# Third layer, head-pair scores: one fp32 product against three rounded products of split queries and keys

## The chip, the cores and the metric

The kernel runs on one core of a Trainium2 chip. The metric is the device time of one launch in microseconds (us). The core has TensorE (PE, matrix products; PEld is its weight load), VectorE (DVE), ScalarE (ACT), GpSimd (POOL) and the queues that issue DMAs (SP). Each engine works through its own instructions in order and waits on semaphores that others raise.

## What is computed

Three layers over 512 tokens of width 1024 (a gated linear attention, a sparse attention, and a hybrid layer with stick-breaking attention). The change is in the third layer's attention, which the reference computes so, in 16 heads of 64 dimensions:

```python
proj = h @ w_in
q, k, v, z_a, u, z_b, m_a, m_b = jnp.split(proj, offs, axis=-1)
...
z = jnp.einsum('bhqd,bhkd->bhqk', qb, kb).astype(jnp.float32) * SB_SCALE
mask = k_pos < q_pos
log_1m_beta = jnp.where(mask, -jax.nn.softplus(z), 0.0)
suffix = lax.cumsum(log_1m_beta, axis=3, reverse=True) - log_1m_beta
w = jnp.where(mask, jnp.exp(jax.nn.log_sigmoid(z) + suffix), 0.0)
outs.append(jnp.einsum('bhqk,bhkd->bhqd', w.astype(vb.dtype), vb))
...
p_a = (attn * jax.nn.silu(z_a)) @ w_branch_a
```

## The kernel before

**Products.** Every large matrix product is three products of rounded parts: both operands are split into a high part (rounded to the type fp32r) and a low part (what is left of it), and high x high, high x low and low x high are added up in PSUM. Weights come in chunks of 256 columns, numbered c; ACT rounds the high part (`split_high`), POOL subtracts it for the low part (line 600). The third layer's chunks start at C_H = 40: four chunks each for a group of four heads, q, k, v, z; from C_MA = 56 on come other columns. A chunk's product has two halves m = 0 and 1 of 24 matmuls with 512 columns each (line 1224), or 48 with 256 (line 1215, for v).

**Two banks for the products.** During the head pairs the products of all chunks share PSUM banks 0 and 1, half m in bank m (`shared=True`). So half m of chunk c + 1 must not start before half m of chunk c has been taken out of the bank. The semaphores `bank_free` say that; in the kernel before, the take by ACT (`taker`, lines 1084 to 1095) raises them.

**The pairs.** The heads run in 8 pairs p = 0 to 7. Beside pair p, PE computes two chunks of a later group, q and k in the even pairs 0, 2, 4, then v and z in the odd ones 1, 3, 5 (pairs 6 and 7 have chunks of m_a). The order on PE in one pair is written by hand: the pair's scores with their masks (`head_scores`), both halves of chunk c, half 0 of chunk c + 1, the sums of the logarithms (`head_sums`, line 1760), half 1 of chunk c + 1, and the products with the values (`head_values`, line 1774). The two heads of a pair sit in partitions 0 to 63 and 64 to 127, so each score matmul uses 64 rows, and the two heads use different rows of the array. A head's scores are four blocks of keys st = 0 to 3 with 512, 384, 256 and 128 query columns. They are plain fp32: the profile shows two matmuls for each one written.

**What DVE and ACT do beside it.** For each pair: DVE caps the scores in three groups (line 2290), ACT takes Exp and Ln of each (1111, 1114), then DVE makes for each group a maximum, a rounding and a low part (lines 2294 to 2296), on whose last one `head_sums` waits. Behind these DVE makes the low part of the last pair's output (`pair_part`, line 2284) and multiplies this pair's values by the gate (line 2301). The outputs of pair p live in `br_hi[:, p]` and `br_lo[:, p]`, which nothing uses before the pair is done.

Of the kernel before, what the change touches and what calls it, by code (L numbers as in the profile page):

```python
# [14 lines left out]
F32 = mybir.dt.float32  # L15
F32R = mybir.dt.float32r
# [4 lines left out]
P = 128  # L21
D = 1024
S = 512
# [14 lines left out]
NG, NHG, NDH = 4, 4, 64  # L38
# [33 lines left out]
def build_program(nc, A, out):  # L72
    es = ExitStack()
    with es:
        mem = [nc.sbuf_base + 64 - nc.sbuf_base % 64]

        def sb(name, shape, dt=F32):

            n = 1
            for x in shape[1:]:  # L80
                n *= x
            n *= 4
            t = nc.alloc_sbuf_tensor_at(name, list(shape), dt, offset=mem[0])
            mem[0] += (n + 31) // 32 * 32
            assert mem[0] <= nc.sbuf_usable_end, (name, mem[0], nc.sbuf_usable_end)
            return t

        def sem(name):
            return es.enter_context(nc.semaphore(name))

        banks = es.enter_context(nc.psum_tensor("banks", [P, 8, S], F32))
        bank = [banks[:, i, :] for i in range(8)]
# [143 lines left out]

        mem[0] = arena
        br_hi, br_lo = sb("br_hi", [P, KT, S], F32R), sb("br_lo", [P, KT, S], F32R)
        qh, kh = sb("qh", [P, 2, 2, S]), sb("kh", [P, 2, 2, S])
        vh, zh = sb("vh", [P, 2, TT, CW]), sb("zh", [P, 2, 2, S])  # L240
        mix_a = sb("mix_a", [P, KT, S])

# [14 lines left out]
        rows3 = over("rows3", [P, 2, D], qh)  # L257
# [10 lines left out]
        bank_full = [sem(f"bank_full{i}") for i in range(4)]  # L268
        bank_free = [sem(f"bank_free{i}") for i in range(4)]
# [43 lines left out]
        z_full, zc_ready, e_ready, l_ready, sp_ready = sem("z_full"), sem("zc_ready"), sem("e_ready"), sem("l_ready"), sem("sp_ready")  # L313
        mix_sigmoid = sem("mix_sigmoid")
        a2_scored = sem("a2_scored")
        tri_full, w_ready, hv_full, head_gated = sem("tri_full"), sem("w_ready"), sem("hv_full"), sem("head_gated")
        pair_high, pair_low = sem("pair_high"), sem("pair_low")
        d_ready, d_high, d_low, mix_full, mix_taken = sem("d_ready"), sem("d_high"), sem("d_low"), sem("mix_full"), sem("mix_taken")
# [10 lines left out]
        C_H, C_MA, C_U, C_BA, C_ZB, C_MB, C_MIX, C_BB, C_OUT = 40, 56, 60, 64, 68, 72, 76, 77, 81  # L329
# [20 lines left out]
        def blocks(x, a, st, skip=0):  # L350

            at, c0 = zone(a, st)
            return x[:, at, c0 + skip * P:c0 + (TT - st) * P]
# [5 lines left out]
        z_banks = banks[:, 3:8, :]  # L359
# [295 lines left out]
        def _(act):  # L655
# [55 lines left out]
            def step2(c, take, ahead=True):  # L711
                if ahead:
                    split_high(c + 1, (c + 1) // 2, (c + 1) % 2)
                u = c % 2
                for m in range(2):
                    act.wait_ge(bank_full[2 * u + m], c // 2 + 1)
                    take(m, bank[2 * u + m]).then_inc(bank_free[2 * u + m], 1)
# [341 lines left out]
            for u in range(NUNIT + 1):  # L1059
# [4 lines left out]
                q = z_piece_end(u)  # L1064
# [4 lines left out]
                if u in split_next:  # L1069
                    c = split_next[u]  # L1070
# [11 lines left out]
            def taker(c):  # L1082

                s, kind = (c - C_H) // 4 % 2, (c - C_H) % 4
                if c >= C_MA:
                    return lambda m, b: act.activation(mix_a[:, 2 * (c - C_MA) + m], b, ACT.Copy)
                return (lambda m, b: act.activation(qh[:, s, m], b, ACT.Copy, scale=NDH ** -0.5),
                        lambda m, b: act.activation(kh[:, s, m], b, ACT.Copy),
                        lambda m, b: act.activation(vh[:, s, 2 * m:2 * m + 2], b.rearrange("p (t n) -> p t n", t=2), ACT.Copy),
                        lambda m, b: act.activation(zh[:, s, m], b, ACT.Silu))[kind]  # L1090

            def take3(c, m):
                b = 2 * (c % 2) + m
                act.wait_ge(bank_full[b], c // 2 + 1)
                taker(c)(m, bank[m]).then_inc(bank_free[b], 1)

            def pair_split(p):
                act.wait_ge(head_gated, p + 1)
                act.activation(br_hi[:, p], gated[:, p % 2], ACT.Copy).then_inc(pair_high, 1)

            for c in range(C_H, C_H + 4):
                step2(c, taker(c), ahead=(c > C_H))
            for p in range(HH // 2):
                c = C_H + 4 + 2 * p
                if p % 2 == 0:
# [55 lines left out]
            for c in range(C_OUT, C_END):  # L1161
                if c + 1 < C_END:
                    split_high(c + 1, (c + 1) // 2, (c + 1) % 2)
                j = c - C_OUT
# [9 lines left out]
        def _(pe):  # L1174
# [175 lines left out]
            for t in range(TT):  # L1350
                pe.wait_ge(start_scaled, t + 1)
                for k in range(KT):
                    mm = pe.transpose(start_bank(k)[:, t * P:(t + 1) * P], xn_tok[:, t, k * P:(k + 1) * P], ident[:])
# [109 lines left out]
            for h in range(GH):  # L1463
                if h < GH - 1:
                    updates(h + 1)
                for e in range(2):
# [76 lines left out]
            for k in range(KT):  # L1543
# [3 lines left out]
                mm = pe.matmul(bank[2 * u + 1][:], w_hi[:, u, k, 0:2 * NDH], act_hi[:, k, :], start=(k == 0), stop=(k == KT - 1))  # L1547
# [9 lines left out]
            for g in range(NG):  # L1557
                for m in range(2):
                    mm = pe.matmul(bank[6][:, g * NDH:(g + 1) * NDH],
                                   hid4[:, m, g * P:(g + 1) * P],  # L1560
                                   w2v[:, m, :], start=(m == 0), stop=(m == 1))
            mm.then_inc(cmp_full, 1)
            pe.wait_ge(gates_t_ready, 1)
            for t in range(TT):
                mm = pe.matmul(bank[7][:, t * 48:(t + 1) * 48], gate_parts[:, t * P:(t + 1) * P], pair_ident[:], start=True, stop=True)
# [108 lines left out]
            for j in range(2):  # L1674
                c = C_NQ + 2 + j
# [3 lines left out]
            c = C_NZ  # L1679
# [3 lines left out]
            c = C_NZ + 1  # L1683
# [22 lines left out]
            for row, col in enumerate((gain_mod, mod)):  # L1706
                for k in range(KT):
                    mm = pe.matmul(bank[mod_row_bank(row, k // 4)][:, k % 4 * P:(k % 4 + 1) * P],
                                   col[:, k:k + 1].broadcast_to([P, P]), ident[:], start=True, stop=True)
# [7 lines left out]
            def rows3(a):  # L1717
                return slice(a * NDH, (a + 1) * NDH)

            def score(p, a, st, start):  # L1720

                s, tile = p // 2 % 2, p % 2
                return pe.matmul(blocks(z_banks, a, st), kh[rows3(a), s, tile, st * P:(st + 1) * P],  # L1723
                                 qh[rows3(a), s, tile, st * P:S], start=start, stop=False, skip_group_check=True)

            def score_mask(a, st):

# [3 lines left out]
            def head_scores(p):  # L1731

                if p:
                    pe.wait_ge(w_ready, 3 * p)
                score(p, 0, 2, start=True).then_inc(a2_scored, 1)
                score(p, 1, 1, start=True)
                score(p, 0, 1, start=True)
                pe.wait_ge(a2_scored, p + 1)
                score(p, 1, 2, start=False)
                score(p, 0, 3, start=False)  # L1740
                score(p, 1, 3, start=False)
                for st in (1, 3):
                    score_mask(0, st)
                    mm = score_mask(1, st)
                mm.then_inc(z_full, 1)
                score_mask(0, 2)
                score_mask(1, 2).then_inc(z_full, 1)
                score(p, 0, 0, start=True)
                score(p, 1, 0, start=True)
                score_mask(0, 0)  # L1750
                score_mask(1, 0).then_inc(z_full, 1)

# [27 lines left out]
            for p in range(HH // 2):  # L1780
                c = C_H + 4 + 2 * p
# [11 lines left out]
            c, u = C_MIX, C_MIX % 2  # L1793
# [4 lines left out]
            for tile in range(KT):  # L1798
                if tile >= 4:
                    pe.wait_ge(mix_taken, tile - 3)  # L1800
                for i in range(2):
                    k = tile // 2 * 2 + i
                    for n, (w, x) in enumerate(((w_hi, br_hi), (w_lo, br_hi), (w_hi, br_lo))):
                        mm = pe.matmul(bank[4 + tile % 4], w[:, u, k, tile % 2 * P:(tile % 2 + 1) * P], x[:, k, :],  # L1804
                                       start=(i == 0 and n == 0), stop=(i == 1 and n == 2))
# [19 lines left out]
        def _(dve):  # L1825
# [456 lines left out]
            def pair_part(p):  # L2282
                dve.wait_ge(pair_high, p + 1)
                dve.tensor_tensor(br_lo[:, p], gated[:, p % 2], br_hi[:, p].bitcast(F32), ALU.subtract).then_inc(pair_low, 1)

            for p in range(HH // 2):
                for i, g in enumerate((1, 2, 0)):

                    dve.wait_ge(z_full, 3 * p + i + 1)
                    dve.tensor_scalar(group(ln_z, g), group(z_banks, g), CAP, None, ALU.min).then_inc(zc_ready, 1)  # L2290
                for i, g in enumerate((1, 2, 0)):

                    dve.wait_ge(l_ready, 3 * p + i + 1)
                    link(dve.tensor_tensor(group(ln_z, g), group(ln_z, g), group(z_banks, g), ALU.max))
                    link(dve.tensor_copy(group(sp_hi, g), group(ln_z, g)))
                    dve.tensor_tensor(group(sp_lo, g), group(ln_z, g), group(sp_hi, g).bitcast(F32),
                                      ALU.subtract).then_inc(sp_ready, 1)
                if p:
                    pair_part(p - 1)
                dve.wait_ge(hv_full, p + 1)  # L2300
                dve.tensor_tensor(gated[:, p % 2], bank[2], zh[:, p // 2 % 2, p % 2], ALU.mult).then_inc(head_gated, 1)  # L2301
            pair_part(HH // 2 - 1)
# [144 lines left out]
```

## Time and profile before

| | us |
|---|---|
| median of 3 runs | 1287.04 (1286.7 to 1287.11) |
| the profiled execution | 1288.17 |
| its span, first to last instruction | 1286.5 |
| PE busy | 1241.5 (97%) |
| DVE busy | 647.8 (50%) |
| ACT busy | 574.5 (45%) |
| POOL busy | 350.7 (27%) |
| the 8 head pairs in the trace | 736.5 to 1002.9 |

Around the span lie 1288.17 - 1286.5 = 1.7 us. PE's records overlap: a matmul's record is longer than the step to the next one, since its end lies about 0.16 us behind the last column; steps between starts tell the rate.

### The profile page before, as it was taken

Reading aid. Unit: us, or ns where it says so; the run is one execution under the profiler, and the core shown is the slowest. Engines: PE = TensorE matmul, PEld = TensorE weight load, DVE = VectorE, ACT = ScalarE, POOL = GpSimd, SP = SyncE. Lnnn points to the kernel's source line nnn. Section 1 sums busy time; section 2 is a strip of 40 time slices with the busy share of each in tenths; the row PEclk is TensorE's granted clock in tenths of the full one; section 3 lists DMA queues with packets and bytes.
Section 4 is the critical chain, followed back from the end, with each engine's and each line's share of the span. In section 5 each row is a group of like instructions: output and inputs, shape, how many; then the busy total and the mean of one; then the engine's idle time right before and its main releaser. Section 6 shows DMA issues by size and latency. Waiting matters only on the chain.

```text
span 1286.5 us, 19286 instructions
## 1 busy us (share of the span) xinstructions
PE 1241.5 (97%) x7710; PEld 1031.7 (80%) x7710; DVE 647.8 (50%) x1214; ACT 574.5 (45%) x1082; POOL 350.7 (27%) x174
## 2 busy tenths in 40 slices
PE   7999998999899999999999999999999999999998
PEld 6799876998878765566799888788877788888897
DVE  4487544475756657798837033333333491102434
ACT  4434212353532256788845445444444311434333
POOL 3344401210014302100020432322222454444441
PEclk9999997999999999999999999999999999999999
DMA  7326400816566412100022322222222223333221
GB/s 225 119 67 196 131 1 33 261 44 193 153 123 123 103 33 66 25 11 2 2 67 66 99 66 66 66 66 66 66 67 66 66 98 98 98 109 103 77 89 66
DMA packets 131201, 111.69 MB, mean 87 GB/s; under 512 B 38802, under 2 KB 128016, under 8 KB 131120
## 3 DMA queue, kind: packets, MB, share of 16 engines
q1 hardware_dynamic: 129600, 106.84, 28.3%
q10 hardware_dynamic: 1520, 3.72, 1.3%
q8 instruction: 57, 0.93, 0.3%
q14 instruction: 24, 0.20, 0.0%
HBM read 104.78 MB, written 2.10 MB: 83 GB/s over the span
## 4 chain that ended last, share of the span: by engine, by line
PE 71%; issue 14%; DVE 7%; POOL 4%; ACT 3%; DMA 0%; ACTq 0%; POOLq 0%; SPq 0%; DVEq 0%
PE banks L1224 33%; PE banks L1215 8%; PE banks L1247 5%; POOL w_lo L600 4%; PE banks L1760 3%; PE banks L1612 3%; PE banks L1629 3%; PE banks L1644 3%; PE banks L1312 2%; PE banks L1667 2%; PE banks L1723 2%; DVE w_lo L1863 2%; PE banks L1774 1%; PE banks L1804 1%; PE banks L1191 1%
## 5 line engine op out<-in xcount | busy, mean ns | idle before, releaser
L600 POOL TENSOR_TENSOR w_lo<-raw,w_hi 128x1024 fp32r<-128x1024 f32 x138 | 339.8, 2483 | 844.7 <-ACT w_hi L675 832.6
L1224 PE MATMUL banks<-act_hi,w_hi 128*128 128x512 f32 x704 | 278.4, 395 | 5.0 <-DVE w_lo L1863 4.9
L1224 PE MATMUL banks<-act_hi,w_lo 128*128 128x512 f32 x704 | 276.1, 392 | 0.0
L1224 PE MATMUL banks<-act_lo,w_hi 128*128 128x512 f32 x704 | 276.0, 392 | 0.0
L675 ACT ACTIVATE w_hi<-raw 128x1024 fp32r<-128x1024 f32 (+1 forms) x164 | 162.8, 1042 | 134.6 <-PE banks L1224 87.8
L1224 PEld LDWEIGHTS banks<-act_hi,w_hi 128*128 128x128 f32 x704 | 133.3, 189 | 34.3 <-issue 6.3
L1224 PEld LDWEIGHTS banks<-act_lo,w_hi 128*128 128x128 f32 x704 | 133.3, 189 | 28.2
L1224 PEld LDWEIGHTS banks<-act_hi,w_lo 128*128 128x128 f32 x704 | 133.4, 189 | 27.3
L1215 PE MATMUL banks<-w_hi,act_hi 128*128 128x256 f32 x384 | 109.1, 284 | 0.0
L1215 PE MATMUL banks<-w_hi,act_lo 128*128 128x256 f32 x384 | 108.7, 283 | 0.0
L1215 PE MATMUL banks<-w_lo,act_hi 128*128 128x256 f32 x384 | 108.7, 283 | 0.0
L1039 ACT ACTIVATE prob<-prob,wstat 128x128 f32<-128x128 f32 (+3 forms) x128 | 70.8, 554 | 34.0 <-DVE wstat L2192 33.8
L2301 DVE TENSOR_TENSOR tmp<-banks,zh 128x512 f32<-128x512 f32 x8 | 5.5, 692 | 141.7 <-PE banks L1774 141.7
L1215 PEld LDWEIGHTS banks<-w_hi,act_hi 128*128 128x128 f32 x384 | 73.7, 192 | 0.2 <-issue 0.2
L1215 PEld LDWEIGHTS banks<-w_lo,act_hi 128*128 128x128 f32 x384 | 73.7, 192 | 0.0
L1215 PEld LDWEIGHTS banks<-w_hi,act_lo 128*128 128x128 f32 x384 | 73.7, 192 | 0.0
L1629 PEld LDWEIGHTS banks<-ident,prob 128*128 128x128 f32 x320 | 35.7, 141 | 33.1 <-issue 25.2
L1247 PE MATMUL banks<-w_hi,act_hi 128*128 128x256 f32 x192 | 56.2, 293 | 4.7 <-POOL w_lo L600 2.5
L2192 DVE CUSTOM_DVE_ANT_0 prob<-banks,key_mask 128x128 f32<-128x128 f32 (+3 forms) x128 | 57.0, 482 | 3.6 <-PE banks L1612 3.4
L1247 PE MATMUL banks<-w_lo,act_hi 128*128 128x256 f32 x192 | 55.5, 289 | 0.0
L1247 PE MATMUL banks<-w_hi,act_lo 128*128 128x256 f32 x192 | 55.4, 289 | 0.0
L1629 PE MATMUL banks<-ident,prob 128*128 128x128 f32 x320 | 48.1, 280 | 5.7 <-ACT probT L1052 3.7
(380 smaller groups left out, 2405.5 us busy)
## 6 DMA issues: line engine op xcount, KB each, us to landing
raw<-w_in SPq DMA_DIRECT2D x32, 1024.0 KB, 5.7
raw<-gla_w_in SPq DMA_DIRECT2D x11, 1024.0 KB, 5.3
raw<-nsa_w_in SPq DMA_DIRECT2D x33, 256.0 KB, 4.4
raw<-nsa_w_in SPq DMA_DIRECT2D x6, 1024.0 KB, 5.7
raw<-gla_w_out SPq DMA_DIRECT2D x4, 1024.0 KB, 10.2
ada_first<-w_ada SPq DMA_DIRECT2D x4, 1024.0 KB, 9.1
raw<-nsa_w_out SPq DMA_DIRECT2D x16, 256.0 KB, 4.4
raw<-w_branch_a SPq DMA_DIRECT2D x4, 1024.0 KB, 5.1
```

The costliest lines, as they stand in the source:

```text
L600: pool.tensor_tensor(w_lo[:, u, k], raw[:, u, k], w_hi[:, u, k].bitcast(F32), ALU.subtract).then_inc(lo_done, 1)
L675: act.activation(w_hi[:, u, k, 0:n], raw[:, u, k, 0:n], ACT.Copy).then_inc(hi_done, 1)
L1039: act.activation(p, p, ACT.Exp, scale=-1.0, bias=wstat[:, u % 4, 0, half:half + 1], accum_out=wstat[:, u % 4, 1, half:half + 1]).then_inc( ...
L1215: mm = pe.matmul(b[:, t * CW:(t + 1) * CW], x[:, k, tok], w[:, u, k, :], start=(k == 0 and n == 0), stop=(k == KT - 1 and n == 2))
L1224: mm = pe.matmul(b[:], w[:, u, k, m * P:(m + 1) * P], x[:, k, :], start=(k == 0 and n == 0), stop=(k == KT - 1 and n == 2))
L1247: mm = pe.matmul(zone, x[:, k, tok], w[:, u, k, :], start=(start and n == 0), stop=(stop and n == 2), skip_group_check=True)
L1312: mm = pe.matmul(bank[2 * u + m][:, tok], w[:, u, k, m * P:(m + 1) * P], x[:, k, tok], start=(half == 0 and k == 0 and n == 0), stop=(k == ...
L1612: mm = pe.matmul(bank[2 * (u % 2) + half][:, 0:keys], qT[rows, i, t * P:(t + 1) * P], kT[rows, i // 4, 0:keys], start=True, stop=True)
L1629: mm = pe.transpose(bank[4 + half][:, k * P:(k + 1) * P], prob[:, u % 3, half, k * P:(k + 1) * P], ident[:])
L1644: mm = pe.matmul(bank[6][half * NDH:(half + 1) * NDH, 0:P], v_tok2[:, k, w, g * NDH:(g + 1) * NDH], probT[:, u % 2, half, k * P:(k + 1) * ...
L1760: mm = pe.matmul(blocks(z_banks, a, st, skip=jt - st), (tri_r if jt == st else minus_r)[:], blocks(part, a, jt), start=False, stop=(jt == ...
L2192: last = dve.tensor_tensor_reduce(prob[:, u % 3, half, 0:keys], bank[2 * (u % 2) + half][:, 0:keys], key_mask[:, S - keys:S], -1.0, -NEG, ...
```

## The change

`qh` and `kh`, the queries and keys of a group of four heads, are now fp32r, so ACT rounds them as it takes them from the banks. DVE makes the low parts from the same bank: bank times the scale minus `qh` into `br_hi[:, p]`, bank minus `kh` into `br_lo[:, p]`, in the tiles where the pair's own output will come later. A score block is then three fp32r matmuls (n = 0, 1, 2): high keys with high queries, high keys with low queries, low keys with high queries. The banks of q and k are given free by DVE's instruction, no longer by ACT's, which raises the new semaphore `qk_high`. The low parts of the first group are made before pair 0, those of the later groups during pairs 0, 2 and 4: the queries' two halves behind the pair's softplus chain, the keys' two halves behind `pair_part`.

```diff
-        qh, kh = sb("qh", [P, 2, 2, S]), sb("kh", [P, 2, 2, S])
+        qh, kh = sb("qh", [P, 2, 2, S], F32R), sb("kh", [P, 2, 2, S], F32R)
...
-                taker(c)(m, bank[m]).then_inc(bank_free[b], 1)
+                taken = qk_high if (c - C_H) % 4 < 2 and c < C_MA else bank_free[b]
+                taker(c)(m, bank[m]).then_inc(taken, 1)
...
-            def score(p, a, st, start):
+            def score(p, a, st, n, start):
...
+                k = (kh[:, s, tile], kh[:, s, tile], br_lo[:, p])[n]
+                q = (qh[:, s, tile], br_hi[:, p], qh[:, s, tile])[n]
+                return pe.matmul(blocks(z_banks, a, st), k[rows3(a), st * P:(st + 1) * P], q[rows3(a), st * P:S],
+                                 start=(start and n == 0), stop=False, skip_group_check=True)
...
+                for n in range(3):
+                    mm = score(p, 0, 2, n, start=True)
+                    score(p, 1, 1, n, start=True)
+                mm.then_inc(a2_scored, 1)
+                score(p, 0, 1, 0, start=True)
                 pe.wait_ge(a2_scored, p + 1)
...
+            def query_low(j, m, b):
+
+                dve.wait_ge(qk_high, 4 * j + m + 1)
+                dve.scalar_tensor_tensor(br_hi[:, 2 * j + m], b, NDH ** -0.5, qh[:, j % 2, m].bitcast(F32), ALU.mult,
+                                         ALU.subtract).then_inc(bank_free[2 * (C_H % 2) + m], 1)
+
+            def key_low(j, m, b):
+
+                dve.wait_ge(qk_high, 4 * j + m + 3)
+                dve.tensor_tensor(br_lo[:, 2 * j + m], b, kh[:, j % 2, m].bitcast(F32), ALU.subtract)                    .then_inc(bank_free[2 * ((C_H + 1) % 2) + m], 1)
...
+                if p % 2 == 0 and p < 6:
+                    for m in range(2):
+                        query_low(p // 2 + 1, m, bank[m])
                 if p:
                     pair_part(p - 1)
+                if p % 2 == 0 and p < 6:
+                    for m in range(2):
+                        key_low(p // 2 + 1, m, bank[m])
                 dve.wait_ge(hv_full, p + 1)
```

How the instructions stand on DVE in pair 2, from the last group of the softplus chain (ln_z, sp_hi, sp_lo) on, first in the kernel before. `tmp` is the tile of the gated values.

```order
L2294 TENSOR_TENSOR ln_z_154<-ln_z_154,banks 128x1024 [waits l_ready]
L2295 CAST sp_hi_155<-ln_z_154 128x1024 [waits dve_chain]
L2296 TENSOR_TENSOR sp_lo_163<-ln_z_154,sp_hi_155 128x1024 [waits dve_chain]
L2284 TENSOR_TENSOR br_lo_148<-tmp_62,br_hi_147 128x512 [waits pair_high]
L2301 TENSOR_TENSOR tmp_62<-banks,zh_152 128x512 [waits hv_full]
```

The same place in the changed kernel:

```order
L2326 TENSOR_TENSOR ln_z_154<-ln_z_154,banks 128x1024 [waits l_ready]
L2327 CAST sp_hi_155<-ln_z_154 128x1024 [waits dve_chain]
L2328 TENSOR_TENSOR sp_lo_163<-ln_z_154,sp_hi_155 128x1024 [waits dve_chain]
L2306 SCALAR_TENSOR_TENSOR br_hi_147<-banks,qh_149 128x512 [waits qk_high] x2
L2301 TENSOR_TENSOR br_lo_148<-tmp_62,br_hi_147 128x512 [waits pair_high]
L2312 TENSOR_TENSOR br_lo_148<-banks,kh_150 128x512 [waits qk_high] x2
L2339 TENSOR_TENSOR tmp_62<-banks,zh_152 128x512 [waits hv_full]
```

The two queries' low parts stand behind the whole chain, the two keys' between `pair_part` and the gate.

On PE, the scores of a pair up to the first product of chunk c, in the kernel before (a shape is array columns x moving columns):

```order
L1723 MATMUL banks<-qh_149,kh_150 128x256 [waits bank_free2,bank_free1,bank_free3,bank_free0,consts3_ready]
L1723 MATMUL banks<-qh_149,kh_150 128x384 x2
L1723 MATMUL banks<-qh_149,kh_150 128x256 [waits a2_scored]
L1723 MATMUL banks<-qh_149,kh_150 128x128 x2
L1729 MATMUL banks<-maskb3_161,identb3_160 128x128 x6
L1723 MATMUL banks<-qh_149,kh_150 128x512 x2
L1729 MATMUL banks<-maskb3_161,identb3_160 128x128 x2
```

And in the changed kernel, the first block of the scores, as far as its blocks of 384 and 256 columns go:

```order
L1733 MATMUL banks<-qh_149,kh_150 128x256 [waits bank_free2,bank_free1,bank_free3,bank_free0,consts3_ready]
L1733 MATMUL banks<-qh_149,kh_150 128x384
L1733 MATMUL banks<-br_hi_147,kh_150 128x256
L1733 MATMUL banks<-br_hi_147,kh_150 128x384
L1733 MATMUL banks<-qh_149,br_lo_148 128x256
L1733 MATMUL banks<-qh_149,br_lo_148 128x384
L1733 MATMUL banks<-qh_149,kh_150 128x384
L1733 MATMUL banks<-qh_149,kh_150 128x256 [waits a2_scored]
L1733 MATMUL banks<-br_hi_147,kh_150 128x384
L1733 MATMUL banks<-br_hi_147,kh_150 128x256
L1733 MATMUL banks<-qh_149,br_lo_148 128x384
L1733 MATMUL banks<-qh_149,br_lo_148 128x256
```

The heads alternate, and the wait on `a2_scored` now stands behind the third product of head 0's 256-column block. The first matmul of half 0 of chunk c + 1 waits on lo_done and bank_free0 in both kernels; what differs is who raises bank_free0.

## Rows read from the trace of the kernel before

**Rows 1.** The page: busy time (share of the span) and instructions of each engine
```profile
PE 1241.5 (97%) x7710; PEld 1031.7 (80%) x7710; DVE 647.8 (50%) x1214; ACT 574.5 (45%) x1082; POOL 350.7 (27%) x174
```

**Rows 2.** The chain that ended last, pair 2: start us, us, what
```profile
822.98 5.54 PE banks L1760 x40
...
834.00 2.31 PE banks L1774 x16
836.31 1.60 PE banks L1723 x10
```

**Rows 3.** PE's waits over the whole span: us in total, times, longest (cut)
```profile
PE banks L1723 <- ACT zh L1090: 0.8, 1, 0.8
```

**Rows 4.** Timeline of PE, pair 2's scores: start us, us, engine, line, tiles, shape
```profile
803.18 1.67 PE L1723 MATMUL banks<-qh,kh 64*128 64x256 f32 x12
804.78 0.51 PE L1729 MATMUL banks<-maskb,identb 128*128 128x128 bf16 x6
805.22 1.13 PE L1723 MATMUL banks<-qh,kh 64*128 64x512 f32 x4
806.28 0.28 PE L1729 MATMUL banks<-maskb,identb 128*128 128x128 bf16 x2
```

**Rows 5.** Timeline of PE, the second half of the 512-column block
```profile
805.75 0.60 PE L1723 MATMUL banks<-qh,kh 64*128 64x512 f32 x2
```

**Rows 6.** Timeline of PE, head_sums of pair 1: fp32r matmuls of four widths
```profile
791.38 0.27 PE L1760 MATMUL banks<-sp_lo,minus_r 128*128 128x128 f32 x1
791.49 0.33 PE L1760 MATMUL banks<-sp_hi,tri_r 128*128 128x256 f32 x1
...
792.86 0.28 PE L1760 MATMUL banks<-sp_lo,minus_r 128*128 128x256 f32 x1
792.98 0.34 PE L1760 MATMUL banks<-sp_hi,tri_r 128*128 128x384 f32 x1
...
794.20 0.33 PE L1760 MATMUL banks<-sp_lo,minus_r 128*128 128x384 f32 x1
794.37 0.39 PE L1760 MATMUL banks<-sp_hi,tri_r 128*128 128x512 f32 x1
794.60 0.40 PE L1760 MATMUL banks<-sp_lo,tri_r 128*128 128x512 f32 x1
```

**Rows 7.** Timeline of DVE, pair 2's chain
```profile
805.22 2.95 DVE L2290 TENSOR_SCALAR ln_z<-banks 128x1024 f32<-128x1024 f32 x3 [1.23 <-PE banks L1729]
...
817.13 1.23 DVE L2296 TENSOR_TENSOR sp_lo<-ln_z,sp_hi 128x1024 fp32r<-128x1024 f32 x1
818.27 0.68 DVE L2284 TENSOR_TENSOR br_lo<-tmp,br_hi 128x512 fp32r<-128x512 f32 x1
```

**Rows 8.** Timeline of ACT and PE where chunk c + 1 of pair 2 starts
```profile
812.14 0.60 ACT L1087 ACTIVATE qh<-banks 128x512 f32<-128x512 f32 x1 [0.45 <-PE banks L1224]
...
817.38 0.39 PE L1224 MATMUL banks<-act_hi,w_hi 128*128 128x512 f32 x1
817.58 0.60 ACT L1087 ACTIVATE qh<-banks 128x512 f32<-128x512 f32 x1 [4.32 <-PE banks L1224]
```

**Rows 9.** Groups of DVE by form: xcount | busy us, mean ns | idle before
```profile
L2070 DVE SCALAR_TENSOR_TENSOR rope_q<-banks,cosT 128x512 f32<-128x512 f32 x10 | 6.9, 687 | 5.4 <-PE banks L1224 4.8 <-DVE rope_q L2071 0.5
```

**Rows 10.** Timeline, DVE releases a waiting PE
```profile
692.75 1.22 DVE L2274 TENSOR_TENSOR y_tok<-y_tok,mod_rows 128x1024 f32<-128x1024 f32 x1
...
694.03 0.33 PE L1300 MATMUL banks<-ident,y_tok 128*128 128x128 f32 x1 [0.72 <-DVE y_tok L2274]
```

**Rows 11.** Stretches around pauses of PE: us, busy (x) of five engines, PEclk, DMA share, GB/s
```profile
270.40:272.20 1.80, 0.14 (x2) 0.05 (x1) 1.80 (x4) 1.49 (x7) 0.00 (x0) 1.00 0.11 13
272.20:275.60 3.40, 3.40 (x28) 3.40 (x29) 3.06 (x4) 3.34 (x7) 0.00 (x0) 1.00 0.91 301
299.10:301.10 2.00, 0.14 (x3) 0.08 (x2) 1.39 (x2) 1.52 (x2) 0.00 (x0) 1.00 0.56 127
301.10:304.60 3.50, 3.50 (x9) 2.74 (x10) 3.25 (x6) 0.00 (x0) 0.00 (x0) 0.53 0.32 70
```

More of the change, by code:

```diff
@@ L315, in build_program @@
         a2_scored = sem("a2_scored")
+        qk_high = sem("qk_high")
         tri_full, w_ready, hv_full, head_gated = sem("tri_full"), sem("w_ready"), sem("hv_full"), sem("head_gated")
@@ L1099, in pair_split @@
                 act.activation(br_hi[:, p], gated[:, p % 2], ACT.Copy).then_inc(pair_high, 1)
-            for c in range(C_H, C_H + 4):
-                step2(c, taker(c), ahead=(c > C_H))
+            for c in range(C_H, C_H + 2):
+                if c > C_H:
+                    split_high(c + 1, (c + 1) // 2, (c + 1) % 2)
+                for m in range(2):
+                    act.wait_ge(bank_full[2 * (c % 2) + m], c // 2 + 1)
+                    taker(c)(m, bank[2 * (c % 2) + m]).then_inc(qk_high, 1)
+            for c in range(C_H + 2, C_H + 4):
+                step2(c, taker(c))
             for p in range(HH // 2):
@@ L1718, in rows3 @@
                 return slice(a * NDH, (a + 1) * NDH)
-            def score(p, a, st, start):
+            def score(p, a, st, n, start):
                 s, tile = p // 2 % 2, p % 2
-                return pe.matmul(blocks(z_banks, a, st), kh[rows3(a), s, tile, st * P:(st + 1) * P],
-                                 qh[rows3(a), s, tile, st * P:S], start=start, stop=False, skip_group_check=True)
+                k = (kh[:, s, tile], kh[:, s, tile], br_lo[:, p])[n]
+                q = (qh[:, s, tile], br_hi[:, p], qh[:, s, tile])[n]
+                return pe.matmul(blocks(z_banks, a, st), k[rows3(a), st * P:(st + 1) * P], q[rows3(a), st * P:S],
+                                 start=(start and n == 0), stop=False, skip_group_check=True)
             def score_mask(a, st):
@@ L1734, in head_scores @@
                     pe.wait_ge(w_ready, 3 * p)
-                score(p, 0, 2, start=True).then_inc(a2_scored, 1)
-                score(p, 1, 1, start=True)
-                score(p, 0, 1, start=True)
-                pe.wait_ge(a2_scored, p + 1)
-                score(p, 1, 2, start=False)
-                score(p, 0, 3, start=False)
-                score(p, 1, 3, start=False)
+                for n in range(3):
[3 more added lines that the diff above has]
+                score(p, 0, 1, 0, start=True)
+                pe.wait_ge(a2_scored, p + 1)
+                for n in range(3):
+                    if n:
+                        score(p, 0, 1, n, start=True)
+                    score(p, 1, 2, n, start=False)
+                for n in range(3):
+                    for a in range(2):
+                        score(p, a, 3, n, start=False)
                 for st in (1, 3):
@@ L1747, in head_scores @@
                 score_mask(1, 2).then_inc(z_full, 1)
-                score(p, 0, 0, start=True)
-                score(p, 1, 0, start=True)
+                for n in range(3):
+                    for a in range(2):
+                        score(p, a, 0, n, start=True)
                 score_mask(0, 0)
@@ L2284, in pair_part @@
                 dve.tensor_tensor(br_lo[:, p], gated[:, p % 2], br_hi[:, p].bitcast(F32), ALU.subtract).then_inc(pair_low, 1)
+            def query_low(j, m, b):
[6 more added lines that the diff above has]
+            for m in range(2):
+                query_low(0, m, bank[2 * (C_H % 2) + m])
+            for m in range(2):
+                key_low(0, m, bank[2 * ((C_H + 1) % 2) + m])
             for p in range(HH // 2):
@@ L2297, in _ @@
                                       ALU.subtract).then_inc(sp_ready, 1)
+                if p % 2 == 0 and p < 6:
+                    for m in range(2):
+                        query_low(p // 2 + 1, m, bank[m])
                 if p:
                     pair_part(p - 1)
+                if p % 2 == 0 and p < 6:
+                    for m in range(2):
+                        key_low(p // 2 + 1, m, bank[m])
                 dve.wait_ge(hv_full, p + 1)
```

## The prediction

> **What bounds the kernel now.** I read the page first, then the chain of work that ended last, then PE's waits, then the timelines of all engines in one head pair. PE is busy for 97% of the span, the next engine for 50% [rows 1]. In the chain, a whole pair is PE and nothing else; the three rows shown are pair 2's sums, its values and the scores of the next pair [rows 2], and the other seven pairs repeat this. Of all waits of PE, one lies at the head pairs: 0.8 us for the last z half ahead of pair 0 [rows 3]. So in these 266 us every PE column counts, and nothing else does until it makes PE wait. Two questions follow: how long are the scores on PE, and does a new wait arise.
>
> **The scores on PE.** In pair 2 they stand in two blocks. The first runs from 803.18 to the masks at 804.78, 1.60 us; the 512-column one from 805.22 to 806.28, 1.06 us [rows 4]. Together 2.66 us.
>
> Before: a score is two matmuls, and from the first pair of 512-column ones (805.22) to the second (805.75) are 0.53 us [rows 4, 5]. The two heads start together (two matmuls in one row of the timeline), so they run side by side. Of the 1.06 us, 512 columns take four column times (4 x 512 / 2.4 = 853 ns at the granted full clock of 2.4 GHz), and some 0.2 us are left: the first load of weights and the drain before the masks, which use the whole array. I split them 0.10 and 0.10.
>
> After: three fp32r matmuls for each. The steps between fp32r matmuls on 128 rows are 0.11 us for 128 columns, 0.12 for 256, 0.17 for 384, 0.23 for 512 [rows 6]. No fp32r matmul on 64 rows with two heads side by side is in the trace, so this is to be bounded.
> - 512-column block: 3 x 0.227 + 0.20 = 0.88 us, against 1.06: 0.17 less.
> - First block: the heads go 256 beside 384, then 384 beside 256, then 128 beside 128. In step with the longer one that is 6 x 0.173 + 3 x 0.11 = 1.37, plus 0.20 for load and drain: 1.57. The wait on a2_scored comes on top: it stands behind the third 256-column product, whose record ends 0.28 us after its start (as at 792.86 [rows 6]), and a fresh load of 0.10 follows. Head 0 runs ahead in the meantime (256 columns beside 384), so I count at most 0.1 for it. 1.6 to 1.7 us against 1.60: no change to 0.1 more.
>
> So I take 0.2 us less for the scores of a pair, nearly all in the second block, and none before the first masks, on which DVE's chain waits.
>
> Bounds: at best pure columns. Three column times in place of four make 0.21 us less in the 512-column block and, for 768 columns of a head, 0.32 less in the first: 0.53. At worst the heads don't run side by side: 2 x 3 x (0.227 + 0.173 + 0.12 + 0.11) = 3.8 us plus 0.2 to 0.4, 1.3 to 1.5 more than now. I take the middle estimate since the fp32 rows show both heads in step on the same rows of the array.
>
> One published rule speaks against the gain. The trace has the second 512-column matmul of the same rows starting 0.53 us after the first, of which 0.43 are columns and 0.10 is the first load, so the second load cost nothing [rows 5]. The Trainium skill, "TensorE: Matmul & The Clock Gate", Part 3 (The mechanism), has a load overlap a running matmul only when its row group differs; by that each of the 12 products of a head would show its load.
>
> **The added wait.** In the changed kernel, half 0 of chunk c + 1 waits for bank 0, and in pairs 0, 2 and 4 it is DVE's low part of the queries that gives it free. Before, ACT did: it took q's half 0 at 812.14 to 812.74, and PE wanted the bank at 817.38, 4.6 us later [rows 8]. But on DVE query_low is queued behind the pair's whole softplus chain. Pair 2's chain begins at 805.22 with the first masks, and its last instruction ends at 817.13 + 1.23 = 818.36 [rows 7]. The next instruction of DVE starts at 818.27, a little before that end, and takes 0.68; query_low takes its place. Its duration: 0.687 us for the same operation out of PSUM [rows 9], as long as the low part whose place it takes (0.68); I take 0.69. It ends at 818.96. A waiting PE starts 0.05 us after DVE's end (692.75 + 1.22 = 693.98 with the digits cut off, and 694.03 [rows 10]), and the load, hidden in the stream, now shows with 0.10. So the product that started at 817.38 starts streaming at 819.11: 1.73 us late. What hid ACT's take was 4.6 us of cover; what DVE's place in the queue leaves is less than none.
>
> This time is counted from the pair's first masks, so what the 512-column block saves is swallowed in these three pairs: PE comes to the bank 0.2 us sooner and waits 1.9. In pairs 0 and 4 the chain stands the same way (the odd ones have no query_low).
>
> Who waits behind it: everything on PE, whose queue is in order; nothing of that is recovered, since PE is the bound to the end. head_sums finds its inputs ready: they were 4.6 us early (818.36 against 822.98 [rows 2, 7]) and now more.
>
> **The other waits.** query_low of half 1 needs ACT's take, 817.58 to 818.18 [rows 8], which is there by 818.96; it ends at 819.65, and bank 1 is wanted only after half 0 and head_sums, 11 us on. key_low of half 0 comes while PE is in head_sums. key_low of half 1 waits for the half that ends with line 1224 at 834.00, then 0.6 for ACT's take and 0.7 of its own: done 1.3 us after, where the gate on DVE waits for head_values, 2.31 us [rows 2]: covered by 1.0. The next pair's chunk needs these banks 3 us later still. The first group's four low parts lie before pair 0, beside 22 us of v and z products; DVE is idle there. ACT's rounding costs it 0.03 us each, with ACT at 45%. All of this at nothing; if key_low were not covered it would push the gate of three pairs by some 0.3 us, still behind PE.
>
> **The sum.** Three pairs with +1.73: +5.2. Five pairs with -0.2: -1.0. Together +4.2 us, from 1288.17 to 1292.4 for the profiled execution, and from the median 1287.04 to 1291.2. The profiled one lies 1.1 above the median, all of it kept out of the difference.
>
> **The clock.** PE pauses for 1.9 us three times in a stretch where it never paused. What such pauses do to the granted clock shows in the second layer: after that from 270.4 it stayed at full, after that from 299.1 it stood at 0.53 of full for 3.5 us, near the lower of its two levels [rows 11]. 3.4 us at half speed lose 1.7. [...]
>
> **Rivals.**
> 1. As summed, no clock fall: +4.2, 1291.2 us. Range of its own 1290.2 to 1292.2.
> 2. One of the three pauses brings the clock down: +5.9, 1292.9. Two or three: +7.6 to +9.3, up to 1296.3. For it: one of the two pauses of this length in rows 11. Against: it was the longer one.
> 3. The scores gain in full, and the stall shrinks with them: the first masks come 0.32 sooner, so the chain and the bank too. 3 x (1.73 - 0.32) - 5 x 0.53 = +1.6, 1288.6: not slower than can be told. It decides at a first block of 1.3 us in place of 1.6. For it: a fourth of the column time is really gone. Against: the 0.11 us step at 128 columns [rows 6] and the wait on a2_scored.
> 4. Each product shows the load of its weights, 0.10. In the first block the nine steps have columns for 6 x 0.16 + 3 x 0.05 = 1.12 us, with nine loads and the drain 2.1, so 0.5 more; the second has 3 x (0.21 + 0.10) + 0.10 = 1.04, as now. 3 x (1.73 + 0.5) + 5 x 0.5 = +9.2, 1296.2. Against: rows 5. It is what the rule on loads above would give.
> 5. The heads run one after another: 3 x (1.73 + 1.0) + 5 x 1.3 = +14.7, 1301.7.
> 6. The wait isn't there: only if DVE took the bank ahead of its chain, which the order of its instructions rules out. It would leave 8 x -0.2 = -1.6, 1285.4.
>
> **Chances.** First 0.48; second 0.32 (one fall 0.23, more 0.09); third 0.09; fourth 0.05; fifth 0.03; sixth 0.03. The forecast is 1291.2 us. A measurement of this kernel tells 0.2%, 2.6 us, from no change: 1289.6 is the bound. Slower: 0.48 + 0.32 + 0.05 + 0.03 = 0.88. Same: the third and nearly all of the sixth, 0.11. Faster: 0.01, the far end of the sixth. The range 1289.4 to 1294.8 holds the first and one or two clock falls.
>
> **What would show it.** PE's waits get a line of 1224's successor on DVE's query_low (line 2306), 3 times, 1.7 to 1.9 us each, and head pairs 0, 2 and 4 last 1.7 longer, the others 0.2 shorter. In the stretch of each pair the first block of scores reads 1.5 to 1.7 us, the 512-column one about 0.9. query_low reads 0.69 and starts as the last low part of the chain ends. I am wrong if there is no such wait, if the first block's length is off by more than 0.2, or if the clock falls behind a pause.

## The result: 0.3% slower, by the wait on DVE's queue

| | kernel before | changed kernel |
|---|---|---|
| median | 1286.7 us (13 runs) | 1290.87 us (13 runs) |
| ratio to before | | 1.0029, 95% interval 1.0018 to 1.0040 |
| profiled execution: time, span | 1288.17, 1286.5 | 1289.53, 1287.8 |
| from pair 0's first score to the first matmul behind pair 7 | 266.33 | 270.18 |
| from there to the end | 283.66 | 283.65 |

The forecast was +4.2 us; the medians differ by 4.2, the ratio says 3.7 (2.3 to 5.1), so that the two 4.2 agree to the digit is luck. The two profiled spans differ by only 1.3 us. This is no smaller loss: the eight pairs alone take 3.85 us longer, and the stretch behind them is the same to 0.01. What is missing lies ahead of pair 0, which starts at 736.46 in one trace and at 733.96 in the other. Matmul by matmul, this distance is complete at 506 us, ahead of the third layer, and changes by less than 0.05 us from there to pair 0. So the first group's low parts, which the changed kernel makes there, cost nothing. The distance comes for the most part from the clock, which stood at half for 30.7 us of the first two layers in one trace and for 23.9 in the other. In all traces below that front part moves by some us from run to run, while the last part is 283.65 to 283.67. So I take effects from the eight pairs, and the ratios beside them.

A wait of PE in the changed kernel that the kernel before hasn't (us in total, times, longest us):

```profile
PE banks L1232 <- DVE br_hi L2306: 5.0, 3, 1.7
```

Line 1232 is the chunks' product (before: 1224), line 2306 the low part of the queries. In the kernel before only the 0.8 us of [rows 3] lay at the pairs.

The chain that ended last, in pair 2 of the changed kernel (start us, us, what):

```profile
802.22 1.51 PE banks L1733 x17
803.73 0.34 PE banks L1739 x4
804.08 0.02 issue
804.10 2.96 DVE ln_z L2322 x3
...
816.01 1.23 DVE sp_lo L2328
817.24 0.61 DVE br_hi L2306
817.85 0.04 issue
817.89 5.74 PE banks L1232 x24
```

Where [rows 2] had PE alone, the chain now leaves PE at the first masks, runs through the whole softplus chain on DVE and ACT and comes back through the queries' low part. The timelines of DVE and PE there:

```profile
816.01 1.23 DVE L2328 TENSOR_TENSOR sp_lo<-ln_z,sp_hi 128x1024 fp32r<-128x1024 f32 x1
817.15 1.28 DVE L2306 SCALAR_TENSOR_TENSOR br_hi<-banks,qh 128x512 fp32r<-128x512 f32 x2
818.35 2.49 DVE L2301 TENSOR_TENSOR br_lo<-tmp,br_hi 128x512 fp32r<-128x512 f32 x1
```
```profile
815.85 0.39 PE L1232 MATMUL banks<-act_lo,w_hi 128*128 128x512 f32 x1
817.89 0.50 PE L1232 MATMUL banks<-act_hi,w_hi 128*128 128x512 f32 x1 [1.66 <-DVE br_hi L2306]
```

The low part starts 13.05 us behind the start of the chain at 804.10, as the low part of line 2284 does in [rows 7] (818.27 - 805.22), and PE starts streaming 0.05 us after its first half is done (two halves in 1.28 us, 0.68 each, since they overlap a little). The scores of the same pair:

```profile
802.15 0.44 PE L1733 MATMUL banks<-qh,kh 64*128 64x256 f32 x2
...
803.66 0.51 PE L1739 MATMUL banks<-maskb,identb 128*128 128x128 bf16 x6
804.10 0.50 PE L1733 MATMUL banks<-qh,kh 64*128 64x512 f32 x2
804.44 0.39 PE L1733 MATMUL banks<-br_hi,kh 64*128 64x512 f32 x2
804.67 0.39 PE L1733 MATMUL banks<-qh,br_lo 64*128 64x512 f32 x2
805.00 0.28 PE L1739 MATMUL banks<-maskb,identb 128*128 128x128 bf16 x2
```

The first block takes 803.66 - 802.15 = 1.51 us (1.60 in [rows 4]), the 512-column one 0.90 (1.06). From the second to the third product are 0.23 us, the step of 128-row fp32r matmuls in [rows 6]. "x2" are the two heads.

The length of the eight pairs, from start to start, in us:

| pair | 0 | 1 | 2 | 3 | 4 | 5 | 6 | 7 | sum |
|---|---|---|---|---|---|---|---|---|---|
| before | 33.03 | 33.69 | 33.06 | 33.69 | 33.06 | 33.69 | 33.06 | 33.06 | 266.33 |
| changed | 34.76 | 33.44 | 34.73 | 33.44 | 34.77 | 33.44 | 32.78 | 32.82 | 270.18 |

Pairs 0, 2 and 4 are 1.73, 1.67 and 1.71 longer, the others 0.24 to 0.28 shorter: +5.1 and -1.3.

### The profile page after: what moved, and what is told of

Its sections match the earlier page's. It is cut to its first block, busy times and chain, and to the rows that moved or that the text cites. A ratio compares the mean times of both kernels' runs of the same rounds, so it can differ in the third digit from the quotient of the medians.

```text
span 1287.8 us, 19430 instructions
## 1 busy us (share of the span) xinstructions
PE 1236.9 (96%) x7774; PEld 1030.1 (80%) x7774; DVE 662.1 (51%) x1230; ACT 574.5 (45%) x1082; POOL 351.2 (27%) x174
## 4 chain that ended last, share of the span: by engine, by line
PE 68%; issue 14%; DVE 9%; POOL 4%; ACT 4%; ACTq 1%; DMA 0%; SPq 0%; POOLq 0%; DVEq 0%
PE banks L1232 31%; PE banks L1223 8%; PE banks L1255 5%; POOL w_lo L601 4%; PE banks L1777 3%; PE banks L1620 3%; PE banks L1637 3%; PE banks L1652 3%; PE banks L1320 2%; PE banks L1675 2%; DVE w_lo L1880 2%; PE banks L1791 1%; PE banks L1733 1%; PE banks L1821 1%; ACT w_hi L676 1%
```

## The experiments

Eight further runs: six new kernels, one of them twice, and the changed kernel again. Ratios are to the kernel before on the same chip. Its median there was 1287.6 us for the first four rows and 1287.24 us for the last four.

| kernel | eight pairs, us | against before | median | ratio, 95% interval |
|---|---|---|---|---|
| low part of the queries early | 264.34 | -2.0 | 1284.96 | 0.9979 (0.9967 to 0.9991) |
| the wait alone, old scores | 271.66 | +5.3 | 1292.72 | 1.0043 (1.0030 to 1.0057) |
| low part later | 273.00 | +6.7 | 1292.64 | 1.0040 (1.0026 to 1.0054) |
| early, heads apart | 269.60 | +3.3 | 1291.3 | 1.0034 (1.0017 to 1.0050) |
| the changed kernel again | 270.18 | +3.9 | 1290.78 | 1.0035 (1.0023 to 1.0048) |
| early, again | 264.29 | -2.0 | 1288.02 | 0.9996 (0.9979 to 1.0013) |
| early, no score wait | 263.58 | -2.7 | 1284.77 | 0.9982 (0.9969 to 0.9994) |
| early, heads in threes | 263.70 | -2.6 | 1282.13 (one run) | |

### The low part of the queries ahead of the last group

```diff
                     dve.tensor_tensor(group(sp_lo, g), group(ln_z, g), group(sp_hi, g).bitcast(F32),
                                       ALU.subtract).then_inc(sp_ready, 1)
-                if p % 2 == 0 and p < 6:
-                    for m in range(2):
-                        query_low(p // 2 + 1, m, bank[m])
+                    if i == 1 and p % 2 == 0 and p < 6:
+                        query_low(p // 2 + 1, 0, bank[0])
+                if p % 2 == 0 and p < 6:
+                    query_low(p // 2 + 1, 1, bank[1])
```

> The changed kernel with one instruction of VectorE moved: in pairs 0, 2 and 4 the low part of the queries' half 0 stands ahead of the last of the three groups of the softplus chain, no longer behind it. Everything else is as in the changed kernel. Theory A (the place in VectorE's queue is the whole loss): the low part ends 3.4 us sooner, well ahead of the product that wants bank 0; the three pauses of TensorE of 1.66 us go, the chain ends 0.7 us later and head_sums, which has over 4 us to spare, doesn't notice. The head pairs lose 3 x 1.7 = 5 us against the changed kernel and stand at 8 x -0.26 = -2.1 against the kernel before, ratio 0.9984. Rival B (the loss lies in VectorE's added work itself, or in its reads of the banks beside TensorE): as much work, so the ratio stays near 1.003. Rival C (the chain's delay moves the wait to head_sums): a wait at head_sums takes its place, ratio 1.000 or more.

DVE's timeline in pair 2, and PE's where half 0 of chunk c + 1 starts:

```profile
813.62 0.68 DVE L2306 SCALAR_TENSOR_TENSOR br_hi<-banks,qh 128x512 fp32r<-128x512 f32 x1
814.22 1.21 DVE L2326 TENSOR_TENSOR ln_z<-ln_z,banks 128x1024 f32<-128x1024 f32 x1
...
817.93 2.53 DVE L2301 TENSOR_TENSOR br_lo<-tmp,br_hi 128x512 fp32r<-128x512 f32 x1
```
```profile
815.46 0.39 PE L1232 MATMUL banks<-act_lo,w_hi 128*128 128x512 f32 x1
815.68 0.39 PE L1232 MATMUL banks<-act_hi,w_hi 128*128 128x512 f32 x1
```

The low part ends at 814.30, the product starts at 815.68 one step of 0.22 us behind the last. PE has no wait on line 2306 any more and none on the sums; its chain in pair 2 is all PE again:

```profile
801.79 1.51 PE banks L1733 x15
803.31 0.44 PE banks L1739 x6
803.75 0.90 PE banks L1733 x6
804.65 0.22 PE banks L1739 x2
804.87 16.42 PE banks L1232 x72
```

The same instructions in another place save 5.8 us in the pairs: the place was the loss. The expectation's 5 left out that the three pairs, once their length isn't set by the wait, keep the 0.25 us of the scores too. Rivals B and C fall.

Run again, beside the changed kernel:

> The run with the early low part of the queries once more, beside the changed kernel itself. Theory: 5.5 us less than the changed kernel (in the trace 270.2 against 264.3 us for the eight pairs), 2.1 less than the kernel before, ratio to it 0.998.

The eight pairs took 264.29 us, 5.9 less than the changed kernel's 270.18 beside it. The ratio, 0.9996, isn't the 0.998 expected and doesn't settle it: 6 of its 12 executions lie at 1289.3 to 1289.9 us with a mean clock of 0.984, the others at 1282.6 to 1286.7. The kernel before had such executions too (4 of 23 at 1291.5 to 1291.9 us and 0.985), only not as often; in the traces half-clock stretches ahead of pair 0 make such differences, and why this one met more of them stays open.

### The changed kernel, beside the others

> The changed kernel as it is, on the chip of the next three, so that they can be compared with it. Theory: +3.7 us against the kernel before (ratio 1.003), with the three pauses of 1.66 us in pairs 0, 2 and 4.

It came out at 1.0035, with 270.18 us in the pairs, as in its first trace.

### The wait without the new scores

```diff
-            def score(p, a, st, n, start):
+            def score(p, a, st, start):
 
                 s, tile = p // 2 % 2, p % 2
-                k = (kh[:, s, tile], kh[:, s, tile], br_lo[:, p])[n]
-                q = (qh[:, s, tile], br_hi[:, p], qh[:, s, tile])[n]
...
+                return pe.matmul(blocks(z_banks, a, st), kh[rows3(a), s, tile, st * P:(st + 1) * P].bitcast(F32),
+                                 qh[rows3(a), s, tile, st * P:S].bitcast(F32), start=start, stop=False, skip_group_check=True)
...
```

> The changed kernel with the scores in the old form: one plain fp32 product for each block, in the old order, on the rounded queries and keys. The low parts are still made and still give the banks free, but no product reads them, so the low parts are left out of the scores. Theory A: the wait without the gain. The first masks come as late as before the change, so the pause is shorter on TensorE's side by what the scores no longer save (1.4 us in place of 1.66), and the pairs 0, 2, 4 last 1.73 longer than before, the others the same: +5.2 us against the kernel before, ratio 1.0040. If the score products themselves cost anything hidden, this one would come out faster than the changed kernel; theory A has it 1.3 us slower (5 x 0.25).

```profile
PE banks L1232 <- DVE br_hi L2297: 4.4, 3, 1.5
```

Pairs 0, 2 and 4 last 34.84, 34.83, 34.83 us, 1.8 more than before, the others within 0.02 of before: +5.3 for the wait by itself. Against it the changed kernel has 1.5 less. That is what the new scores are worth while the wait sets the length of three pairs: 5 x 0.25 saved in the others, and in these three the first masks, and with them the chain, come 0.09 sooner (0.06 in pair 0).

### The low part one instruction later

```diff
-                if p % 2 == 0 and p < 6:
-                    for m in range(2):
-                        query_low(p // 2 + 1, m, bank[m])
                 if p:
                     pair_part(p - 1)
+                if p % 2 == 0 and p < 6:
+                    for m in range(2):
+                        query_low(p // 2 + 1, m, bank[m])
```

> The changed kernel with the queries' low parts one instruction later: behind pair_part. Theory A: the pause grows by that instruction's 0.68 us in the two pairs that have one (2 and 4; pair 0 has none), from 1.66 to 2.35, so +1.4 us against the changed kernel, ratio to the kernel before 1.004. If pair_part there runs beside GpSimd's split and takes 2.5 us, as it does in the changed kernel, the pauses of pairs 2 and 4 grow by 2.5 each, +5 us. Rival B: no difference to the changed kernel.

Pairs 0, 2, 4 last 34.78, 36.95 and 35.34 us. Pair 4 is 0.57 longer than in the changed kernel and pair 0, which has no `pair_part`, is the same: the pause follows the place in the queue. The 0.68 of the first theory is nearly met; the 2.5 that it allowed for isn't, since `pair_part` takes 0.68 here (the last section shows why). Pair 2 has 1.6 us more still, which the theory didn't have: +2.8 in all against the changed kernel, not +1.4. The stretches around its pause and pair 4's show why (us; busy of PE, PEld, DVE, ACT, POOL; PEclk; DMA share; GB/s):

```profile
818.10:820.40 2.30, 0.07 (x2) 0.05 (x1) 2.30 (x4) 2.24 (x3) 0.62 (x1) 1.00 0.00 0
820.40:825.00 4.60, 4.60 (x13) 3.67 (x14) 0.50 (x1) 0.24 (x1) 4.07 (x2) 0.63 0.00 0
888.50:890.70 2.20, 0.01 (x1) 0.00 (x0) 2.20 (x4) 2.15 (x3) 0.54 (x1) 1.00 0.00 0
890.70:894.10 3.40, 3.36 (x15) 2.79 (x16) 0.58 (x1) 0.33 (x1) 3.40 (x2) 1.00 0.00 0
```

Behind the pause of 2.2 us in pair 2 the granted clock is 0.63 on the mean of 4.6 us, part of it at the lower level; behind pair 4's pause of the same length it is full. The changed kernel's three pauses of 1.7 us never did this, in either of its two traces, nor the three of 1.5 us in the experiment before. In the changed kernel, pair 2:

```profile
816.20:817.90 1.70, 0.04 (x2) 0.01 (x1) 1.70 (x3) 1.63 (x3) 0.01 (x1) 1.00 0.00 0
817.90:821.30 3.40, 3.40 (x15) 2.83 (x16) 2.94 (x2) 0.86 (x1) 3.40 (x2) 1.00 0.00 0
```

The length of a pause alone doesn't tell what the clock does. In the second layer of the same trace a fall followed a pause of the same 1.7 us:

```profile
461.00:462.70 1.70, 0.16 (x2) 0.17 (x4) 1.48 (x8) 0.18 (x1) 0.00 (x0) 1.00 0.00 0
462.70:467.30 4.60, 4.60 (x19) 3.13 (x20) 2.52 (x17) 3.46 (x16) 0.00 (x0) 0.63 0.01 4
```

### The two heads apart, and in threes

Built on the early low part. All products of head 0 stand ahead of all of head 1, in both blocks:

```diff
-                for n in range(3):
-                    mm = score(p, 0, 2, n, start=True)
-                    score(p, 1, 1, n, start=True)
-                mm.then_inc(a2_scored, 1)
...
+                for n in range(3):
+                    mm = score(p, 0, 2, n, start=True)
+                mm.then_inc(a2_scored, 1)
+                for n in range(3):
+                    score(p, 0, 1, n, start=True)
+                for n in range(3):
+                    score(p, 0, 3, n, start=False)
+                for n in range(3):
+                    score(p, 1, 1, n, start=True)
                 pe.wait_ge(a2_scored, p + 1)
...
-                for n in range(3):
-                    for a in range(2):
+                for a in range(2):
+                    for n in range(3):
                         score(p, a, 0, n, start=True)
```

> As the run with the early low part of the queries, but the scores' products in another order: all of head 0's, then all of head 1's, in both blocks. Theory (the two heads run side by side only where they alternate): the first block takes 2 x 1.21 + 0.2 = 2.6 us in place of 1.51 and the 512-column block 6 x 0.227 + 0.2 = 1.56 in place of 0.90, so 1.75 us more for each pair, 14 us in all, ratio 1.009 against the kernel before. Rival (the order doesn't matter, since TensorE lets a later head's product pass): the same time as the run that it is built on.

Neither held for the first block, which took 2.18 us, not 2.6 and not 1.51; the 512-column block took 0.90, as in alternating order. The eight pairs are 5.3 us longer than with the early low part alone, not 14. The timeline in pair 2:

```profile
802.40 0.33 PE L1733 MATMUL banks<-br_hi,kh 64*128 64x384 f32 x1
802.58 0.33 PE L1733 MATMUL banks<-qh,br_lo 64*128 64x384 f32 x1
802.59 0.44 PE L1733 MATMUL banks<-qh,kh 64*128 64x384 f32 x2
802.81 0.39 PE L1733 MATMUL banks<-br_hi,kh 64*128 64x128 f32 x2
...
804.38 0.51 PE L1733 MATMUL banks<-qh,kh 64*128 64x512 f32 x2
804.72 0.41 PE L1733 MATMUL banks<-br_hi,kh 64*128 64x512 f32 x2
```

Head 0's sixth product starts at 802.58. At 802.59 starts a high x high one of 384 columns: head 1's first, the tenth in the program. Head 0's seventh to ninth, the 128-column ones, come later: the seventh is the other one of the "x2" of that row and starts at 802.75, the eighth has the row at 802.81. In the 512-column block the fourth product of the program starts beside the first (804.38, x2). So a product whose rows of the array are free starts ahead of up to three earlier ones that wait for theirs. It didn't start ahead of four: at 802.40, when head 0's fifth started, the sixth to ninth waited, and so did head 1's first. It is the same in all eight pairs. Head 1 had nothing to do for the first 0.8 us. The Trainium skill, "TensorE: Matmul & The Clock Gate", Part 3 (The mechanism), says that matmuls keep the order of the program in start and end; this trace differs in the starts.

The next kernel tests that with three of one head against three of the other in every block, on the order of the last experiment below:

> As the run without the score wait, but each head's three products of a block stand together, three of head 0, then three of head 1, and so on in all blocks. In the run with the heads apart, the 512-column block had this form and still took 0.90 us, with both heads starting within 0.01 us. Theory (a product of the other row group passes up to three or four earlier ones that wait for their rows): the same block lengths as in the alternating order, about 1.44 and 0.90 us. Rival (products start in program order, and the 512-column block was an exception): head 1 starts 0.24 us or more after head 0 in each block, the first block 1.7 us or more.

```profile
799.14 0.46 PE L1733 MATMUL banks<-qh,kh 64*128 64x256 f32 x2
799.36 0.41 PE L1733 MATMUL banks<-br_hi,kh 64*128 64x256 f32 x2
...
800.56 0.51 PE L1739 MATMUL banks<-maskb,identb 128*128 128x128 bf16 x6
```

First block 1.42 us, second 0.90: the rival falls, at a distance of three the order of the heads doesn't matter.

### The first block without the wait on a2_scored

```diff
-                score(p, 0, 1, 0, start=True)
-                pe.wait_ge(a2_scored, p + 1)
                 for n in range(3):
-                    if n:
-                        score(p, 0, 1, n, start=True)
-                    score(p, 1, 2, n, start=False)
+                    score(p, 0, 1, n, start=True)
+                    score(p, 1, 3, n, start=False)
+                pe.wait_ge(a2_scored, p + 1)
                 for n in range(3):
-                    for a in range(2):
-                        score(p, a, 3, n, start=False)
+                    score(p, 0, 3, n, start=False)
+                    score(p, 1, 2, n, start=False)
```

> The early low part of the queries, and another order of the first block of the scores: head 0's blocks of 256, 384 and 128 columns beside head 1's of 384, 128 and 256, so that head 1 has work while head 0's 256-column block ends and the wait on a2_scored finds it done. Theory: each head has 3 x (0.12 + 0.17 + 0.11) = 1.2 us of work; the first block falls from 1.51 to about 1.44 us, 0.6 us in the eight pairs, ratio to the kernel before 0.9975. Rival (the wait costs nothing, the pairing sets the block): no difference in the block, 1.51.

```profile
805.05 0.45 PE L1733 MATMUL banks<-qh,kh 64*128 64x256 f32 x2
...
806.47 0.51 PE L1739 MATMUL banks<-maskb,identb 128*128 128x128 bf16 x6
806.91 0.50 PE L1733 MATMUL banks<-qh,kh 64*128 64x512 f32 x2
```

The block takes 1.42 us (806.47 - 805.05), 0.1 less than with the wait, and the eight pairs 263.58, 0.7 less than the early low part alone. This is 3 x (0.12 + 0.17 + 0.11) + 0.2 = 1.4, one head's own work with load and drain. The edit changes which blocks run side by side and where the wait stands, both at once. For the wait speaks the changed kernel's trace: behind it both heads start together at 802.84, 0.05 us after their rows are free (802.61 + 0.17 for 384 columns), with records 0.1 us longer than those of the same widths in the stream ahead of it. With 1284.77 us and an interval of 0.9969 to 0.9994 this kernel is 0.2% faster than the kernel before and 0.5% faster than the changed one (1290.78 beside it).

## Why the prediction was right, point by point

- **What bounds:** right. PE had no other wait at the pairs before, and each us of it came through: the part behind the pairs kept its length to 0.02 us in every kernel.
- **The added wait:** 1.73 us late in pairs 0, 2, 4 by the sum, 1.73, 1.67 and 1.71 by the pairs' lengths. query_low started with the end of the chain and took 0.68 where I took 0.69; PE followed in 0.05, as I had it. No experiment shows anything else in it: in an earlier place the wait is gone, in a later one it is longer, and with the old scores the same pairs are 1.8 longer.
- **The scores:** 0.25 less for a pair against 0.2. The 512-column block is the sum's: 0.165 less, 0.17 forecast. The first block was mis-sized: 0.09 less where I had 0 to 0.1 more. The step that failed is "in step with the longer one": the heads don't go in step, each runs through its own 1.2 us, and the order of the program holds one back only where more than three products lie between. The wait on a2_scored at 0.1 fits the 0.09 that the block loses without it, as far as one edit of two things can tell.
- **The rule on loads:** no sign of it. From the second to the third 512-column product of the same rows are 0.23 us, 0.21 of them columns. Rival 4 is out by that, rival 5 by the two heads' common starts, rival 3 by a first block of 1.51 (it needed 1.3), rival 6 by the wait itself.
- **The clock:** the forecast of no fall held for these pauses (1.66 us between records; the 1.9 of the forecast counts from the last column, which lies ahead of a record's end). Nine pauses of 1.5 to 1.7 us (twice three in the changed kernel, three with the old scores) and the first one of the later low part left it at full. With pauses half a microsecond longer the fall I feared came, behind one of two, at 1.6 us where I had 1.7. The prediction held "it was the longer one" against a fall; that was no argument: the kernel before has two more such pauses than [rows 11] shows, and of these the shorter one brought the clock down (1.8 us from 500.6, 0.54 of full clock behind it) and the longer one didn't (2.0 us from 242.7). Why all pauses of this length in the pairs were spared, and so how far it was luck, isn't shown.
- **The other waits:** none arose. One cover was thinner than I said: `pair_part` took 2.49 us, not 0.68. It ended at 820.84, 3.5 us ahead of the keys' half 0 (824.30), so it cost nothing.
- **The sum:** +5.2 - 1.0 = +4.2; in the traces +5.1 - 1.3 = +3.85. The two small misses, 0.1 less loss and 0.25 more gain, point the same way; the medians' 4.2 hides them.

## What to carry to other kernels

When a buffer's release moves to another engine, its price is not the new instruction's length but what stands ahead of it in that engine's queue; find the first waiter and its slack before choosing the place. Here 0.68 us of work cost 1.7 us three times behind a chain and nothing ahead of that chain's last group. Spare time of an engine (DVE at 50%) says nothing about whether an instruction comes in time.

## What the runs showed of the hardware

- **Products of different row groups pass each other.** A score product of the other 64 rows started ahead of three earlier ones in the program that waited for their rows (802.59), but not ahead of four. Two streams on different rows need not be interleaved one by one; within three is enough (first block 1.42 us in threes, 1.42 in alternation).
- **fp32r on 64 rows** keeps the steps of 128 rows (0.23 us for 512 columns), both heads side by side. Three fp32r products in place of one plain fp32 take 0.90 in place of 1.06 us at 512 columns: a gain of 15%, not of a quarter, since load and drain (0.2 us) and a step's overhead stay.
- **VectorE beside GpSimd.** The same subtraction of two SBUF operands took 0.68 us at 818.27 before the change [rows 7] and 2.49 us at 818.35 after it. Before, GpSimd's split began at 819.20, behind it; after, at 817.89, ahead of it, and it took 5.21 us for its two halves in place of 4.74:

```profile
817.89 5.21 POOL L601 TENSOR_TENSOR w_lo<-raw,w_hi 128x1024 fp32r<-128x1024 f32 x2 [10.14 <-ACT w_hi L676]
```

The queries' low parts, which read one operand from PSUM, ran at 0.68 each, the second of them beside GpSimd. The run with the low part one instruction later has `pair_part` ahead of GpSimd again, and it takes 0.68:

```profile
819.02 0.68 DVE L2301 TENSOR_TENSOR br_lo<-tmp,br_hi 128x512 fp32r<-128x512 f32 x1
819.78 4.70 POOL L601 TENSOR_TENSOR w_lo<-raw,w_hi 128x1024 fp32r<-128x1024 f32 x2 [10.16 <-ACT w_hi L676]
```

The Trainium skill, "SBUF — State Buffer", "Summary: rules for kernel authors", says that VectorE with two SBUF inputs and a GpSimd instruction that reads SBUF block each other, the second until the first is done; 817.89 + 2.4 for GpSimd's first half plus 0.6 is about the 820.84 at which this one ended, so the trace agrees.
